# First attention layer: probabilities turned on VectorE and through DRAM instead of on TensorE, values and gate half an item later

## What is computed

```
(a_q, a_ckv, i_q, i_k, i_w, a_gate, b_q, b_k, b_v, b_gate, c_q, c_gate, mix_gate) = split(rmsnorm(x) @ w_in)
oa = dsa_attention(qa, ka, va, iq, ik, iw, bias_a, topk=128) * silu(a_gate)     # 6 heads of 128, causal top-128 keys
ob = sliding_window_attention(qb, kb, vb, sinks, bias_b)     * silu(b_gate)     # 12 heads of 64, band of 128
oc = memory_attention(qc, kc, vc)                            * silu(c_gate)     # 4 heads of 128, 256 memory tokens
merged = g_a * (oa @ w_up_a) + g_b * (ob @ w_up_b) + g_c * (oc @ w_up_c)        # g = sigmoid(mix_gate + bias)
x = x + merged @ w_o
```

## Time and profile before

| | us |
|---|---|
| median of 3 runs | 2534.44 |
| lowest, highest | 2534.25, 2534.82 |
| the profiled execution's own time | 2533.8 |
| its span | 2532.2 |
| PE busy in the span | 2517.8 |
| DVE busy | 1237.1 |
| ACT busy | 745.2 |
| POOL busy | 391.0 |
| granted clock of TensorE, mean share | 0.999 |

### The profile page before, as it was taken

One profiled execution on the slowest core, in us unless ns is written; L12 is line 12 of the kernel. 1 busy time (PEld: TensorE's weight loads), 2 busy tenths in 40 slices (PEclk: granted clock), 3 DMA queues, 4 the chain that ended last, 5 costly groups with the idle time before them and its releaser, 6 DMA issues.

```text
span 2532.2 us, 33395 instructions
## 1 busy us (share of the span) xinstructions
PE 2517.8 (99%) x12420; PEld 2066.6 (82%) x12420; DVE 1237.1 (49%) x2109; ACT 745.2 (29%) x1054; POOL 391.0 (15%) x599
## 2 busy tenths in 40 slices
PE   9999999999999999999999999999999999999998
PEld 7788888888888888888888888888888888888886
DVE  5673222223336875544655333464646455454525
ACT  6422122223333432333322222232323232223221
POOL 0111000000010111111000220122112333343100
PEclk9999999999999999999999999999999999999999
DMA  7547333333353443445544444566665645556622
GB/s 274 172 158 210 125 108 125 116 119 122 121 159 135 150 155 133 162 153 190 178 171 161 140 129 151 186 188 203 198 206 183 201 155 157 177 160 206 238 100 100
DMA packets 90337, 410.09 MB, mean 162 GB/s; under 512 B 16214, under 2 KB 16214, under 8 KB 62150
## 3 DMA queue, kind: packets, MB, share of 16 engines
q1 hardware_dynamic: 38712, 241.58, 27.6%
q0 software_dynamic: 51536, 167.30, 21.3%
HBM read 330.49 MB, written 79.81 MB: 162 GB/s over the span
## 4 chain that ended last, share of the span: by engine, by line
PE 97%; DMA 1%; DVE 1%; SPq 0%; issue 0%; ACT 0%; POOL 0%; DVEq 0%; POOLq 0%; ACTq 0%
PE bank L414 28%; PE bank L415 28%; PE bank L416 28%; PE bank L1163 4%; PE bank L1086 2%; PE bank L1223 2%; PE bank L1065 2%; PE bank L947 1%; PE bank L919 1%; PE bank L928 1%; DMA w_raw<-wst 1%; PE bank L882 1%; PE bank L942 0%; PE bank L914 0%; DMA flip_d<-flip_n 0%
## 5 line engine op out<-in xcount | busy, mean ns | idle before, releaser
L403 DVE TENSOR_TENSOR w_lo<-w_raw,w_hi 128x2048 fp32r<-128x2048 f32 x204 | 469.3, 2300 | 551.4 <-ACT w_hi L398 551.4
L414 PE MATMUL bank<-act_a,w_hi 128*128 128x512 f32 (+1 forms) x1672 | 656.5, 393 | 0.4 <-DVE w_lo L403 0.4
L416 PE MATMUL bank<-act_a,w_hi 128*128 128x512 f32 (+1 forms) x1672 | 651.1, 389 | 0.0
L415 PE MATMUL bank<-act_a,w_lo 128*128 128x512 f32 (+1 forms) x1672 | 650.8, 389 | 0.0
L398 ACT ACTIVATE w_hi<-w_raw 128x2048 fp32r<-128x2048 f32 x203 | 388.6, 1914 | 687.0 <-PE bank L416 604.8
L414 PE MATMUL bank<-act_b,w_hi 128*128 128x512 f32 x1280 | 501.5, 392 | 0.0
L415 PE MATMUL bank<-act_b,w_lo 128*128 128x512 f32 x1280 | 498.4, 389 | 0.0
L416 PE MATMUL bank<-act_b,w_hi 128*128 128x512 f32 x1280 | 498.1, 389 | 0.0
L414 PEld LDWEIGHTS bank<-act_a,w_hi 128*128 128x128 f32 (+1 forms) x1672 | 313.5, 188 | 69.9 <-issue 4.1
L416 PEld LDWEIGHTS bank<-act_a,w_hi 128*128 128x128 f32 (+1 forms) x1672 | 313.5, 187 | 66.2
L415 PEld LDWEIGHTS bank<-act_a,w_lo 128*128 128x128 f32 (+1 forms) x1672 | 313.7, 188 | 63.7
(11 more groups left out here) (319 smaller groups left out, 2225.9 us busy)
## 6 DMA issues: line engine op xcount, KB each, us to landing
w_raw<-wst SPq DMA_DIRECT2D x210, 1024.0 KB, 4.9
prob_t<-flip_d POOLq DMA_DIRECT2D x48, 512.0 KB, 4.6
mix_d<-stage POOLq DMA_DIRECT2D x24, 512.0 KB, 2.9
mixg<-mix_d POOLq DMA_DIRECT2D x8, 1536.0 KB, 6.9
flip_d<-flip POOLq DMA_DIRECT2D x24, 512.0 KB, 3.7
flip_d<-flip_a POOLq DMA_DIRECT2D x16, 512.0 KB, 2.9
b<-rows_2d POOLq DMA_DIRECT2D x16, 448.0 KB, 10.1
raw_m<-wst SPq DMA_DIRECT2D x4, 1024.0 KB, 14.0
```

The costliest lines, as they stand in the source:

```text
L403: dve.tensor_tensor(w_lo[s][:], w_raw[s][:], w_hi[s][:].bitcast(F32), ALU.subtract).then_inc(lo_ready, 1)
L414: pe.matmul(out_ap, l_hi, r_hi, start=start, stop=False)
L415: pe.matmul(out_ap, l_lo, r_hi, start=False, stop=False)
L416: return pe.matmul(out_ap, l_hi, r_lo, start=False, stop=stop)
```

## The change

- PE no longer turns probabilities: `turn`, `turns` and the PSUM copies on VectorE and ScalarE (`turned_dve`, `turned_act`) are gone.
- VectorE turns the 32x32 blocks of two token blocks at a time (`flip1`, h = 0 after quarter 0's softmax, h = 1 after quarter 1's) into `flip_1[h]`.
- POOL stores `flip_1[0]` and `flip_1[1]` (512 KB each) into `flip_d` and loads them back with the blocks exchanged: `prob1_t` (one load, 1 KB runs) and `prob1_tk` (two loads, 512 B runs). The keys stand in the order 4a + j, so v is loaded in that order too.
- The values of an item stand after quarter 1 of the next item's group, the gate on VectorE after that item's `flip1`. The last item's values stand after the last group.
- POOL stores an item's output, and loads the item after next (same buffers), only after that later gate; the flips of the item in hand come behind those loads. In item 16 three parts of `o_raw` are loaded between. Part 3 shares its place with `flip_1` and waits for the last flips.
- `flip_stored`, shared with the second layer, starts from a higher count; `first_d` has 12 rows. The first two items of each kind are written out ahead of the loops, POOL's sixteen items are all written out.

```diff
-            def turn(kind, it, k):
...
-                for b in blocks_of(kind, k):
-                    last = pe.transpose(bank[2 + k][:, b * P:(b + 1) * P], prob[:, k, b * P:(b + 1) * P], ident)
-                last.then_inc(t_ready, 1)
...
             def pv(kind, it, k, v):
 
                 tb = tb_of(k)
-                pe.wait_ge(pt_act if k % 2 else pt_dve, 2 * it + k // 2 + 1)
+                pe.wait_ge(prob1_loaded[k // 2], 32 * it - 16 if k // 2 else 16 * it)
...
                 for hs in range(4):
-                    if hs == turn_part(last):
-                        turns(kind, it)
-                    elif hs == 3:
-                        values(kind, it, par)
                     gemm_part(g, hs, act_a)
-                if not last:
-                    values(kind, it, par)
+                    if hs == 1 and before:
+                        values(before, it - 1, 1 - par)
...
+            def flip1(kind, it, h):
+
+                dve.wait_ge(flip_stored[h], 16 * it - 16)
+                dve.wait_ge(p_ready, 4 * it + (2 * h + 2))
+                dve.nop(nofuse=True)
+                dst = flip_1[h][:].rearrange("p j (n b) -> p n j b", b=32)
+                src = prob[:, 2 * h:2 * h + 2, :].rearrange("p k (n j b) -> p (k n) j b", j=4, b=32)
+                if kind == "B" and h == 0:
+                    last = dve.transpose(dst, src)
...
+            def o_store(it):
+                pool.wait_ge(o_ready, it + 1)
+                pool.dma_start(o_d[it - 2], o_st[it % 2][:]).then_inc(o_out[it % 2], 16)
+
+            def flips_1(it):
+
+                for h in range(2):
+                    pool.wait_ge(flip1_ready, 2 * it + h - 3)
+                    pool.wait_ge(prob1_loaded[h], 32 * it - 48 if h else 16 * it - 16)
+                    pool.dma_start(flip_d[h].ap(), flip_1[h][:]).then_inc(flip_stored[h], 16)
+                pool.wait_ge(pv_ready, it)
+                pool.wait_ge(flip_stored[0], 16 * it)
+                pool.dma_start(prob1_t[:], bass.AP(flip_d[0], 0, [[256, P], [32 * 1024, 4], [1, 256]])).then_inc(prob1_loaded[0], 16)
+                pool.wait_ge(flip_stored[1], 16 * it)
+                for k in range(2):
+                    pool.dma_start(prob1_tk[k][:], bass.AP(flip_d[1], P * k, [[256, P], [32 * 1024, 4], [1, P]])).then_inc(prob1_loaded[1], 16)
...
+            for it in range(2, 18):
+                if it > 2:
+                    o_store(it - 1)
+                    if it < 17:
+                        (next_b if it < 7 else load_c if it < 11 else next_a)(it - 1, (it + 1) % 2)
+                if it == 16:
+                    for s in range(2):
+                        pool.wait_ge(o_out[s], 128)
+                    for p in range(3):
+                        load_part(o_d, PARTS_1, p)
+                flips_1(it)
+                if it < 17:
+                    mix_store(G_MIX + 6 + it, it // 2, it % 2, 6)
```

More of the change, by code:

```diff
@@ L363, in build_kernel @@
         v2a = sem("scale2_chain")
[L364 removed]
+        flip_stored = [sem(f"flipped_stored{i}") for i in range(2)]
         pv2_ready, o2_ready = sem("pv2_psum"), sem("o2_ready")
@@ L634, in _ @@
         def _(pe):
-            for first, n in ((s_ready, 8), (t_ready, 8), (pv_ready, 2), (i_psum, 6), (qssq, 1)):
+            for first, n in ((s_ready, 8), (pv_ready, 2), (i_psum, 6), (qssq, 1)):
                 pe.sem_inc(first, n)
@@ L952, in logits @@
             def logits(kind, it, par):
-                pe.wait_ge(pt_dve, 2 * it)
-                pe.wait_ge(pt_act, 2 * it)
+                pe.wait_ge(l_ready, 4 * it)
                 for k in range(4):
                     qk(kind, it, k, qb1[par], kb1[par])
[L959 to L963, removed]
             def values(kind, it, par):
@@ L968, in values, with mix_item @@
                     pv(kind, it, k, vb1[par])
-            def mix_item(kind, it0, i, par, last=False):
+            def mix_item(kind, it0, i, par, before):
                 it = 2 * i + (it0 + par)
@@ L976, in mix_item @@
                 for hs in range(4):
-                    if hs == turn_part(last):
-                        turns(kind, it)
-                    elif hs == 3:
-                        values(kind, it, par)
                     gemm_part(g, hs, act_a)
-                if not last:
-                    values(kind, it, par)
+                    if hs == 1 and before:
+                        values(before, it - 1, 1 - par)
             pe.wait_ge(i_rel, 54)
+            before = None
             for kind, it0, n in (("B", 2, ITEMS_B), ("C", 8, ITEMS_C), ("A", 12, ITEMS_A)):
-                with pe.Fori(0, n // 2 - (kind == "A")) as i:
+                mix_item(kind, it0, 0, 0, before)
+                mix_item(kind, it0, 0, 1, kind)
+                with pe.Fori(1, n // 2) as i:
                     for par in range(2):
-                        mix_item(kind, it0, i, par)
-            for par in range(2):
-                mix_item("A", 12, ITEMS_A // 2 - 1, par, last=(par == 1))
+                        mix_item(kind, it0, i, par, kind)
+                before = kind
+            values("A", 17, 1)
             UP = ((0, 6, (2, 3)), (6, 10, (0, 1)), (10, 16, (4, 5)))
@@ L1231, in _ @@
         def _(act):
-            for first, n in ((e_ready, 8), (pt_act, 4), (i_rel, 6), (x1h_s, 2), (ev_act, 3)):
+            for first, n in ((e_ready, 8), (i_rel, 6), (x1h_s, 2), (ev_act, 3)):
                 act.sem_inc(first, n)
@@ L1466, in exp, with att_act @@
                                    accum_out=rs[:, k, 0:1]).then_inc(e_ready, 1)
[L1468 to L1479, removed]
+            def att_act(kind, it, hs, sink):
                 if hs < 2:
@@ L1514, in _ @@
                 mix_item("A", 12, ITEMS_A // 2 - 1, par, last=(par == 1))
-            for p in range(2, 4):
-                part_hi(PARTS_1, p, 1)
+            act.wait_ge(pv_ready, 18)
+            part_hi(PARTS_1, 2, 1)
+            act.wait_ge(o_ready, 18)
+            part_hi(PARTS_1, 3, 1)
             split_hi(act, 2 * G_UP + 1, 1)
@@ L2070, in att_dve, with mix_item @@
                     soft_b(kind, it, 2 * hs + 1)
-                elif hs == turn_part(last):
-                    turned_dve(kind, it, 0)
-                    turned_dve(kind, it, 2)
-            def mix_item(kind, it0, i, par, last=False):
+                    flip1(kind, it, hs)
+            def mix_item(kind, it0, i, par, gate=True):
                 it = 2 * i + (it0 + par)
@@ L2086, in mix_item @@
                 for hs in range(4):
-                    att_dve(kind, it, hs, lambda: split_lo(dve, 2 * g + 1, 1), last, **kw)
+                    att_dve(kind, it, hs, lambda: split_lo(dve, 2 * g + 1, 1), **kw)
+                    if hs == 1 and gate:
+                        if par:
+                            gated1(i, it0, 0)
+                        else:
+                            gated1(i - 1, it0, 1)
                     if hs == 2:
@@ L2117, in _ @@
                     dve.wait_ge(topk_s, 98)
-                with dve.Fori(0, n // 2 - (kind == "A")) as i:
+                for par in range(2):
+                    mix_item(kind, it0, 0, par, gate=(kind != "B" or par))
+                with dve.Fori(1, n // 2) as i:
                     for par in range(2):
                         mix_item(kind, it0, i, par)
-            for par in range(2):
-                mix_item("A", 12, ITEMS_A // 2 - 1, par, last=(par == 1))
             def part_lo(parts, p, before):
@@ L2129, in part_lo @@
                                   ALU.subtract).then_inc(olo_s, 1)
-            for p in range(4):
+            for p in range(2):
+                part_lo(PARTS_1, p, 0)
+            gated1(2, 12, 1)
+            for p in range(2, 4):
                 part_lo(PARTS_1, p, 0)
```

106 lines of the change are left out of this document (44 added, 62 removed).

## The result

The changed kernel took 2551.16 us (median of six runs, 2545.41 to 2560.51) beside 2534.95 for the kernel before (2534.25 to 2539.52): a ratio of 1.0066, 95% interval 1.0053 to 1.0079. The forecast was 2530.7, and its range ended at 2543. The kernel became slower by 16 us; the case that comes nearest is rival 3, the late loads, at 2553.5.

What follows compares the result with a forecast made beforehand. TensorE's matmuls were taken as the bound, busy 2517.8 us of a 2532.2 us span. 2533.8 - 19.4 + 6.5 + 6.7 + 1.0 + 1.5 = 2530.1, plus 0.6 for the median: 2530.7 us, range 2517 to 2543.

Steps and rivals of the forecast that it cites:

- rival 3: Next item's loads late everywhere, g and bias landing 3 us later than costed: 2553.5 us, chance 0.16.
- What goes: On TensorE, 176 turns (17.8 us) and 16 breaks behind them (1.6 us) vanish: a gain of 19.4 us.
- VectorE: In B items VectorE's work with flips and gate takes 24.7 us against TensorE's 25.5: not the bound.
- Rival 4: Weight splits on VectorE slip and it replaces TensorE as bound, so the gain does not count: about 2534, chance 0.08.
- Loads of the next item: Loads issued behind the later gate land late for B items and item 8: 6.5 us lost.
- bias ring: In B items VectorE cannot start the next item before its bias lands: a 27.2 us cycle against TensorE's 25.5.
- T + 25.9: T is the start of an item's logits; g for the next item lands at T + 25.9, past 25.5.
- C and A, at nothing: Next item's loads in C and A items cost nothing; A's cover is 0.3 to 1.6 us.
- the end: Losses at item 16, the clock and item 17 with the end: 9.2 us.
- Item 16: Its values wait for flips queued behind three parts of `o_raw`: 6.7 us lost, bounds 3 and 10.
- Clock: A TensorE wait of 6 us can fall to half clock: 1 us taken, between 0 and 3.
- Item 17: Its flips follow item 16's late gate, so its values wait: 1.5 us with the end, bounds 0 and 3.

Runs made afterwards that it cites:

- number 9: Changed kernel with the edits of number 7 and Number 6: 2518.55 us; its last kernel adds the later second weight split in B and C items: 2518.50 us.
- number 7: Changed kernel with a separate semaphore for q and k, issued with the bias half an item earlier, ahead of the gate wait: 2521.08 us.
- number 5: Changed kernel with the second weight split behind top-k in B and C, and behind the next item's loads in A (items 12 to 16): 2525.09 us.
- numbers 1 and 2: Changed kernel with flip stores held until the next item's four loads landed: 2549.16 us; with flip stores cut to 32 partitions: 2552.28 us.
- Number 6: The kernel of number 5 with item 16's flip stores and loads ahead of the first three attention output parts: 2521.25 us.
- number 1: Changed kernel with the two flip stores issued only once the next item's four loads have landed: 2549.16 us.
- numbers 1 to 4: Changed kernel, each with one edit: flip stores after loads, 2549.16 us; quarter-size flip stores, 2552.28; plain v order, 2551.93; later second weight split in B and C, 2536.87.
- second look at the changed kernel: The changed kernel run once more, unaltered: 2554.39 us.

## Why the prediction was wrong, step by step

- **What goes (19.4 us): held.** The turns are gone, and TensorE's busy time is 19.4 us under the earlier trace rows in the execution with nearly no waits (2498.4, number 9), 18.5 in number 7. In the changed kernel itself only 11.2 of it shows; some 5 of the rest went to slow-clock matmuls.
- **VectorE: held.** The flips of a half take 1.25 us, or 0.71 and 0.40 in two, as costed from the earlier trace rows; nothing waits for `w_lo` in the stretch. Rival 4 did not come.
- **Loads of the next item: the step that failed.** The prediction had the place right (the weight load goes out beside gb's issue; g due about when the logits are) and mis-sized the landing: 5.4 us, 6.7 at most, where g takes 7.8 to 9.7 us in B. It took 6.7 us from a row where the weight load starts 0.9 us *behind* g, and took off 1.3 for a mixing store that no longer runs ahead. That store had landed at 1019.3, 0.3 us after g's issue at 1019.0, so it was hardly beside g; and in number 5, with no mixing store ahead, g takes as long as it did before with it (4.0 to 5.8 against 3.9 to 5.5 us, the weight load 2 us or more behind in both). What made that row slow was the start of the weight load. In the kernel before alone the loads with the weight load 0.4 to 1.2 us behind took 5.5 to 6.7, those with 3.0 to 4.5 took 3.9 to 5.5; at 1.2 to 0.1 us ahead, a place which that trace does not hold, they take 7.0 to 9.7. The step should have read these rows as one series and gone beyond 6.7, not below it. B then lost 13.3 us, where 6.5 were forecast, and by another path: most of the 6.5 came from the bias ring, while g by the prediction's own sum was only 0.4 us late (T + 25.9 against 25.5).
- **C and A, at nothing: failed with it.** The cover in A was given as 0.3 to 1.6 us, with the warning that each microsecond beyond costs five. g took 7.0 to 8.8 us where 5.4 were costed, and 6.6 us were lost. This is rival 3. Its mechanism (late loads everywhere) is right. Of its two reasons, the weights beside the loads hold, and the flips in the same queue, put first, are excluded by numbers 1 and 2 as the source of the 3 us. That its 2553.5 comes near the time is in part luck: it held 22 us for B (13.3 measured), 7.5 for A (6.6 in C and A) and 9.2 for the end (2.9), and no slow clock in the items, which took 5. Its 0.16 was too little for a place whose worst row left 0.3 us.
- **The bias ring of B: did not bind, but was mis-sized too.** In the changed kernel's B items VectorE stood idle for the logits, not for bb; TensorE's own wait for g came first. bb took 9.0 to 10.2 us in B, not 7.5, and landed only 0.4 to 1.4 us before it was used, so by itself it might have held B nearly as long (not tried). The prediction called 9.0 us the row of the one place with a weight load close behind g. There was a second one, with 0.4 us between (the weight load was issued at 1157.35), and there bb took 10.9:

```profile
L2497 POOL DMA_DIRECT2D gb<-g_d x1: 546/546/546, 1156.9 to 1156.9; - x1
...
DMA to landing us min/median/max: 5.7/5.7/5.7
...
L2515 POOL DMA_DIRECT2D bb<-rows_a x1: 613/613/613, 1157.5 to 1157.5; - x1
...
DMA to landing us min/median/max: 10.9/10.9/10.9
```
- **Item 16: mis-sized.** 1.25 us, where 6.7 were forecast. The two stores landed 13.4 and 14.0 us after their issue, not 19.1 as in the earlier trace rows, whose place had a second weight load beside it. From the first part's issue (1179.6) to the second store's landing (1196.4) it took 16.8 us, and the sum by the earlier trace rows had 21.4. The estimate by the Trainium skill's fixed time and rate ("DMA: Bandwidth & Descriptors", Anatomy of one DMA) had 13.6 for the same stretch (T + 20.4 to T + 34); the trace lies 3.2 us above the page's figure and 4.6 below the row's. Number 6 shows that the order of the queue is worth up to 3.8 us here.
- **Clock: mis-sized.** About 5 us in three items, where one was forecast: behind waits of 3.13, 4.76 and 2.97 us the stretch from logits to values takes 14.4 to 14.5 us and not 12.8 (12.7 in item 8). One long wait was costed, in item 16, where none came; there were three, in items 4, 6 and 8.
- **Item 17: held.** 1.6 us for 1.5.

The sum by measured terms, in spans: 2532.2 - 19.4 + 19.9 (waits for g) + 2.9 (for prob_t) + 5 (clock) = 2540.6; the span is 2545.5. Of the 4.9 left some 2.3 stand around the 12 waits for g, as 0.1 to 0.2 us each. From the start of item 3's logits to the start of item 17's the changed kernel takes 387.4 us and number 9's last kernel 360.2; of these 27.2 us 19.9 are the waits and 5 the clock. The rest I can't place.

## What to carry to other kernels

Before a load is moved to a place where its landing is due at once, list every transfer of the *other* queues that will start beside it, and read the landing from rows with just that neighbour; if no row has it, carry on the series instead of taking something off its worst row. The last transfer of a group sets a semaphore for all of them: give those that are due first (q, k) their own, and issue them before the wait that only the others need. An expected gain on the bound engine that arrives as waits can be had back by order and semaphores: here 33 us lay between the changed kernel (2551.16) and the same kernel with two orders altered and one semaphore split (2518.55).

## What the runs showed of the hardware

**The neighbour in the other queue counts, the follower in the same queue hardly does.** 1 MB on SP's queue at the same instant makes a 256 KB load of POOL's queue 3 us slower, with q, k and v just ahead of it (median 8.1 us in the changed kernel, 4.8 in number 5). 1 MB of stores behind it on its own queue changes its median by 0.1 us and its mean by 0.4 (number 1). What stands ahead of it counts too: with v alone ahead and the weight load 0.9 to 1.0 us behind, g takes 3.4 to 4.8 us (number 7), and with q, k and v ahead and the weight load 0.9 to 1.2 us behind, 5.5 to 6.7 (the kernel before). The Trainium skill states both halves ("DMA: Bandwidth & Descriptors"). A DMA engine takes turns between the queues that have work (Queues, rings and completion order). It begins the work of one queue in its order (Two DMAs through the same engine are not ordered). The trace agrees with what follows from it, by these numbers; the turns themselves no run here shows.

**The clock behind a wait is no fixed price.** In six traces (the changed kernel twice, numbers 1 to 4) the stretch from logits to values kept its full pace within 0.2 us, 12.8 us in B, behind every wait for g up to 1.8 us, and lost 1.4 to 2.7 us behind each of eight waits from 2.9 to 4.8 us, with a granted clock of 0.77 and 0.80 in the windows above, which is part of the time at half (1.2 GHz) and the rest at full (2.4 GHz). Between these two lengths both occur. In the second look at the changed kernel the clock fell with a wait of 2.28 us and stayed with one of 2.73; the windows around the two:

```profile
824.00:828.00 4.00, 1.72 (x9) 1.39 (x10) 0.39 (x1) 3.06 (x3) 0.00 (x0) 0.79 0.94 343
828.00:832.00 4.00, 4.00 (x22) 3.13 (x19) 3.10 (x7) 1.28 (x6) 2.14 (x3) 0.79 0.42 107
...
884.00:888.00 4.00, 2.08 (x18) 1.81 (x19) 0.61 (x2) 2.39 (x3) 0.00 (x0) 1.00 0.70 282
888.00:892.00 4.00, 4.00 (x19) 3.28 (x18) 3.75 (x8) 2.38 (x9) 2.83 (x4) 1.00 0.41 127
```

That may be why the changed kernel's runs lie 15 us apart and number 7's lie 6: more waits of a length that can fall either way. The mean granted clock goes with the time: 0.998 in the fastest of the six runs (2545.41 us), 0.994 in the slowest (2560.51); 0.004 of the span is at most some 10 us (my estimate), so the length of the waits must differ too. This was not tried by itself.
